# TensorE does the up product of the next expert ahead of the down product of the present one

## What is computed

```
logits = hf @ w_router + b_router
top_logit, top_idx = lax.top_k(logits, TOP_K)
top_w = jax.nn.softmax(top_logit, axis=-1)
def expert_block(args):
    gu = xb @ w_gu[e] + b_gu[e]
    g = jnp.minimum(gu[:, :D_EXPERT], SWIGLU_LIMIT)
    lin = jnp.clip(gu[:, D_EXPERT:], -SWIGLU_LIMIT, SWIGLU_LIMIT)
    glu = g * jax.nn.sigmoid(SWIGLU_ALPHA * g)
    return ((lin + 1.0) * glu) @ w_down[e] + b_down[e]
```

## Time and profile before

| | us |
|---|---|
| runs timed | 1204.57, 1202.98, 1203.69; median 1203.69 |
| the profiled execution, its own time | 1205.13 |
| its span, first to last instruction | 1203.3 |
| TensorE busy | 1110.2 |
| VectorE busy, ScalarE busy | 388.4, 266.0 |

### The profile page before, as it was taken

The page is one execution under the profiler, slowest core; times in us unless marked ns, Lnnn a source line. Parts: engine busy times, 40 slices in busy tenths (PEclk is TensorE's granted clock), DMA queues, the critical chain, the costliest instruction groups (busy, mean ns, idle before and its releaser), DMA issues.

```text
span 1203.3 us, 14750 instructions
## 1 busy us (share of the span) xinstructions
PE 1110.2 (92%) x6099; PEld 587.1 (49%) x6099; DVE 388.4 (32%) x655; ACT 266.0 (22%) x402; POOL 4.5 (0%) x10
## 2 busy tenths in 40 slices
PE   9999999999999998889898888989888999988896
PEld 8999999984433333333333333333333333333332
DVE  6768564563222222222222222222222222222223
ACT  5344674432111111111111111111111111111112
POOL 0000000000000000000000000000000000000000
PEclk9999999999999999999999999999999999999999
DMA  9984344589999999999999999999999999999994
GB/s 331 348 279 141 126 162 165 213 319 372 392 436 427 431 430 429 429 431 432 430 429 431 428 431 430 431 430 430 431 430 432 435 412 426 430 429 430 430 425 158
DMA packets 58826, 452.13 MB, mean 376 GB/s; under 512 B 3314, under 2 KB 34279, under 8 KB 40103
## 3 DMA queue, kind: packets, MB, share of 16 engines
q1 hardware_dynamic: 58112, 449.79, 90.8%
q0 software_dynamic: 560, 1.74, 0.5%
q10 hardware_dynamic: 119, 0.08, 0.0%
HBM read 450.53 MB, written 1.06 MB: 375 GB/s over the span
## 4 chain that ended last, share of the span: by engine, by line
PE 50%; DMA 42%; DVE 4%; ACT 1%; issue 1%; SPq 1%; DVEq 0%; ACTq 0%
DMA dring<-in_w_down_dram 35%; PE bank L1069 17%; PE bank L1362 14%; PE bank L1407 14%; DMA ring<-in_w_gu_dram 6%; DVE region_r L1025 1%; DMA ring<-in_w_mem_kv_dram 1%; PE bank L1389 1%; DVE region_r L1022 1%; DVE region_r L1018 1%; PE bank L1300 1%; DVE region_r L1019 1%; PE bank L1270 1%; PE bank L1159 0%; PE bank L1139 0%
## 5 line engine op out<-in xcount | busy, mean ns | idle before, releaser
L1362 PE MATMUL bank<-ring,region_x 128*64 128x512 f32 x2048 | 449.3, 596 | 10.8 <-DMA ring<-in_w_gu_dram 10.8
L1362 PEld LDWEIGHTS bank<-ring,region_x 128*64 128x64 f32 x2048 | 144.5, 137 | 294.9 <-issue 279.6
L1407 PE MATMUL bank<-dring,region_r 128*64 128x512 f32 x1024 | 237.5, 613 | 45.1 <-DMA dring<-in_w_down_dram 44.3
L1407 PEld LDWEIGHTS bank<-dring,region_r 128*64 128x64 f32 x1024 | 71.9, 140 | 196.4 <-issue 128.0
L1018 DVE TENSOR_SCALAR region_r<-bank 128x512 f32<-128x512 f32 x32 | 22.1, 692 | 364.3 <-PE bank L1362 364.3
L1036 DVE SCALAR_TENSOR_TENSOR y_parts<-bank,region_r,y_parts 64x512 fp32r<-64x512 f32 x32 | 23.8, 744 | 324.2 <-ACT y_parts L630 324.2
L621 ACT ACTIVATE region_r<-region_r 128x512 f32<-128x512 f32 x32 | 20.2, 630 | 417.6 <-DVE region_r L1018 417.6
L1069 PE MATMUL bank<-hT_high,w_high 128*128 128x256 f32 x384 | 110.1, 287 | 0.7 <-DVE hT_low L688 0.7
L1069 PE MATMUL bank<-hT_low,w_high 128*128 128x256 f32 x384 | 108.6, 283 | 0.0
L1069 PE MATMUL bank<-hT_high,w_low 128*128 128x256 f32 x384 | 108.6, 283 | 0.0
L696 DVE TENSOR_TENSOR w_low<-ring,w_high 128x2048 fp32r<-128x2048 f32 x39 | 89.3, 2289 | 53.2 <-ACT w_high L470 53.1
(11 more groups left out here) (240 smaller groups left out, 894.9 us busy)
## 6 DMA issues: line engine op xcount, KB each, us to landing
ring<-in_w_gu_dram SPq DMA_DIRECT2D x54, 4096.0 KB, 27.6
dring<-in_w_down_dram SPq DMA_DIRECT2D x58, 2048.0 KB, 24.5
ring<-in_w_gu_dram SPq DMA_DIRECT2D x18, 2048.0 KB, 10.7
ring<-in_w_in_dram SPq DMA_DIRECT2D x26, 1024.0 KB, 11.9
dring<-in_w_down_dram SPq DMA_DIRECT2D x12, 1024.0 KB, 9.5
ring<-in_w_out_dram SPq DMA_DIRECT2D x4, 1024.0 KB, 4.9
ring<-in_w_gu_dram SPq DMA_DIRECT2D x4, 1024.0 KB, 7.6
ring<-in_w_mem_kv_dram SPq DMA_DIRECT2D x3, 1024.0 KB, 11.5
```

The lines of the kernel that those rows point to most:

```text
L1362: last = mm(ps[64 * half:64 * half + 64, :], xg[u // 2][:, c, 64 * (u % 2):64 * (u % 2) + 64], ring[:, slot0 + c, k * F + half * 512:k * F ...
L1407: last = mm(y_ps[64 * half:64 * half + 64, :], lhsT, dring[:, c // 2, at:at + 512], start=(c == 0), stop=(c == KC - 1))
```

## The change

Expert s's down product now stands behind the up product of s+1. The small products of s (`small_products`: transposes of the hidden values, now in `tr_ps`, transposes of the slot matrix, both halves of the scatter) stand inside up(s+1), behind its third chunk. Behind down(s) come both bias rows for up(s+2) and the gather.

SP's order follows. Its first loads are up 3, then down 1 (in two DMAs, not four); then a loop of up(e+2), down(e); at the end up 28 in halves around down 26, then down 27, up 29, down 28, up 30, down 29, down 30, up 31, `b_down`, down 31. TensorE ends with up 30, down 29, small products, down 30, up 31, `b_down`, hidden transposes, down 31, scatter. The mixer's last piece goes to ring slot 12, waits for the attention values (`y_att_sb`), and thereby frees slot 7 one piece earlier.

```diff
@@ -64,7 +63,7 @@
 
-    return (p + 8 - (N_MIX - MIX_RING)) % MIX_RING
+    return MIX_RING if p == N_MIX - 1 else (p + 8 - (N_MIX - MIX_RING)) % MIX_RING
...
@@ -332,9 +331,10 @@
         for j in range(4):
+            if j == 3:
+                sp.wait_ge(y_att_sb, ATT_H // 2 + X_H)
             mixer_piece(p, a["w_out"][0, j * 256:(j + 1) * 256, :].rearrange("(c p) n -> p c n", p=P), 2)
             p += 1
-        sp.wait_ge(y_att_sb, ATT_H // 2 + X_H)
         sp.dma_start(x_again, a["x"][0].rearrange("(t p) d -> p t d", p=P)).then_inc(x_again_in, 16)
 
...
@@ -370,7 +370,7 @@
             sp.wait_ge(pieces_used, used)
             if n < MIX_RING - 8 and n % 2:
                 up_chunks(0, 8 + n - 1, n - 1, 2)
-            elif n % 2:
+            elif n % 2 and n < MIX_RING - 1:
                 up_chunks(1, n - (MIX_RING - 8) - 1, n - (MIX_RING - 8) - 1, 2)
             if used == N_PROJ + 12:
                 down_slots(0, 2, 1)
@@ -378,6 +378,7 @@
                 down_slots(0, 0, 1)
                 down_slots(0, 1, 1)
             if used == N_MIX - 1:
+                up_chunks(1, 6, 6, 2)
                 up_chunks(0, 14, 6, 2)
             if used == N_MIX:
                 up_chunks(0, 12, 4, 2)
@@ -390,37 +391,33 @@
         for m in range(2, KC // 2):
             sp.wait_ge(pieces_used, N_MIX + 2 * m + 2)
             up_chunks(2, 8 + 2 * m, 2 * m, 2)
-        expert_down(1, 1, 1)
         expert_up(3, 0, N_MIX - RING + 25, 2)
-        expert_down(2, 5)
-        with sp.Fori(1, more * (E // 2) + (E // 2 - 1 - IN_ORDER)) as i:
-            expert_up((i * 2 + 2) % E, 8, i * 16 + (N_MIX - RING + 17))
-            expert_down((i * 2 + 1) % E, i * 8 + 1)
-            expert_up((i * 2 + 3) % E, 0, i * 16 + (N_MIX - RING + 25))
+        expert_down(1, 1)
+
+        with sp.Fori(0, more * (E // 2) + (E // 2 - 4)) as i:
+            expert_up((i * 2 + 4) % E, 8, i * 16 + (N_MIX - RING + 33))
             expert_down((i * 2 + 2) % E, i * 8 + 5)
+            expert_up((i * 2 + 5) % E, 0, i * 16 + (N_MIX - RING + 41))
+            expert_down((i * 2 + 3) % E, i * 8 + 9)
...
-        e0 = E - 2 * IN_ORDER
-        sp.wait_ge(pieces_used, ups + e0 * KC + 3)
-        up_chunks(e0, 8, 0, 4)
-        expert_down(e0 - 1, downs + DRING * (e0 - 1))
-        sp.wait_ge(pieces_used, ups + e0 * KC + 7)
-        up_chunks(e0, 12, 4, 4)
-        expert_down(e0, downs + DRING * e0)
-        expert_up(e0 + 1, 0, ups + (e0 + 1) * KC)
-        expert_down(e0 + 1, downs + (e0 + 1) * DRING)
-        with sp.Fori(1, IN_ORDER - 1) as i:
-            for u in range(2):
-                e = i * 2 + (e0 + u)
-                expert_up(e, 8 * (1 - u), ups + e * KC)
-                expert_down(e, downs + e * DRING)
-        expert_up(E - 2, 8, ups + (E - 2) * KC)
-        expert_down(E - 2, downs + (E - 2) * DRING)
-        expert_up(E - 1, 0, ups + (E - 1) * KC, 2)
-        expert_down(E - 1, downs + (E - 1) * DRING, 1)
-
+        sp.wait_ge(pieces_used, ups + (E - 4) * KC + 3)
+        up_chunks(E - 4, 8, 0, 4)
+        expert_down(E - 6, downs + (E - 6) * DRING)
+        sp.wait_ge(pieces_used, ups + (E - 4) * KC + 7)
+        up_chunks(E - 4, 12, 4, 4)
+        expert_down(E - 5, downs + (E - 5) * DRING)
+        expert_up(E - 3, 0, ups + (E - 3) * KC)
+        expert_down(E - 4, downs + (E - 4) * DRING)
+        expert_up(E - 2, 8, ups + (E - 2) * KC, 2)
+        expert_down(E - 3, downs + (E - 3) * DRING, 1)
+        expert_down(E - 2, downs + (E - 2) * DRING, 1)
+        for c, n in ((0, 2), (2, 2), (4, 2), (6, 1), (7, 1)):
+            sp.wait_ge(pieces_used, ups + (E - 1) * KC + c + n - 1)
+            up_chunks(E - 1, c, c, n)
         sp.wait_ge(pieces_used, more * (KC * E) + (KC * (E - 1) + N_MIX))
         sp.dma_start(b_down, a["b_down"][0]).then_inc(b_down_in, 16)
+        expert_down(E - 1, downs + (E - 1) * DRING, 1)
         sp.dma_start(gain_out, a["norm_final_g"].unsqueeze(0).broadcast_to([P, D])).then_inc(final_gain_in, 16)
...
@@ -614,21 +611,44 @@
...
+        sigmoid_of(0)
+        with act.Fori(0, more * E + (E - 2)) as s:
+            hidden(s)
+            slots(s)
+            sigmoid_of(s + 1)
+            weighted_high(s)
+        hidden(more * E + (E - 2))
+        slots(more * E + (E - 2))
+        weighted_high(more * E + (E - 2))
+        slots(more * E + (E - 1))
+        sigmoid_of(more * E + (E - 1))
+        hidden(more * E + (E - 1))
+        weighted_high(more * E + (E - 1))
...
@@ -1007,37 +1027,62 @@
...
+        def expert_steps(i, last_four):
+
+            for u in range(3 if last_four else 4):
+                s = i * 4 + u
+                if not (last_four and u > 1):
+                    dve.wait_ge(gathered, s + 3)
+                    gathered_half(tr_ps, (u // 2 + 1) % 2, u % 2)
+                    if u % 2 and not last_four:
+                        dve.wait_ge(xg_sb, s + 3)
+                        gather_matrices(s + 3)
+                transposed_slots(s, u)
+                scatter_matrix(s + 1)
+                if not (last_four and u > 1):
+                    activations(s + 1)
+                    bias_selector(s + 2)
+                weighted_low(s)
+
+        dve.wait_ge(gathered, 2)
+        gather_matrices(2)
+        activations(0)
+        bias_selector(1)
...
+        with dve.Fori(0, more * (E // 4) + (E // 4 - 1)) as i:
+            expert_steps(i, False)
+        expert_steps(more * (E // 4) + (E // 4 - 1), True)
+        transposed_slots(more * E + (E - 1), E - 1)
+        activations(more * E + (E - 1))
+        weighted_low(more * E + (E - 1))
...
@@ -1331,95 +1376,131 @@
...
+        def begin(s):
+
+            pe.wait_ge(up_read, s + 1)
+            pe.wait_ge(sel_ready, s + 1)
+            bias_rows(0)
+            bias_rows(1)
+
+        def up(i, u, last_one, between):
+
+            s = i * 4 + u
...
+                for k, ps in enumerate((gate_ps, lin_ps)):
+                    for half in range(2):
+                        last = mm(ps[64 * half:64 * half + 64, :], xg[u // 2][:, c, 64 * (u % 2):64 * (u % 2) + 64],
+                                  ring[:, slot0 + c, k * F + half * 512:k * F + half * 512 + 512],
+                                  start=False, stop=(c == KC - 1))
+                last.then_inc(pieces_used, 1)
+                if c == 2:
+                    between()
+
+        def hidden_transposed(s, halves):
+
+            pe.wait_ge(hid_ready, s + 1)
+            pe.wait_ge(xg_sb, s + halves)
+            for c in range(4):
+                last = transpose(tr_ps[:, c * P:(c + 1) * P], g_sb[:, c * P:(c + 1) * P], ident)
+            last.then_inc(hidT_done, 1)
+
+        def slots_and_scatter(s, u):
+
+            pe.wait_ge(y_ready, s + 1)
+            pe.wait_ge(sca_ready, s + 1)
             for t in range(TT):
-                last = transpose(tr_ps[0:E, t * P:(t + 1) * P], wexp[:, t, 0:E], ident)
-            last.then_inc(wexpT_done, 1)
-
-        def four_experts(i, first_four, last_four):
-
+                last = transpose(y_ps[:, t * P:(t + 1) * P], sca[:, t, :], ident)
+            last.then_inc(scaT_done, 1)
+            pe.wait_ge(scaT_sb, s + 1)
+            for t in range(TT):
+                scatter((u + 1) % 2, t, False)
...
+        def down(s, single):
+
+            pe.wait_ge(hidT_sb, s + 2)
+            pe.wait_ge(scaT_sb, s + 2)
+            pe.wait_ge(w_slot_ready, s + 1)
...
+        def next_half(i, u):
+
+            if u % 2 == 0:
+                pe.wait_ge(gat_ready, i * 2 + (u // 2 + 2))
+            gather(tr_ps, u % 2)
...
+        bias_rows(0)
+        up(0, 0, False, second_half)
+        start_sum(1, 1)
+        pe.wait_ge(weights_sb, 1)
+        for t in range(TT):
+            last = transpose(tr_ps[0:E, t * P:(t + 1) * P], wexp[:, t, 0:E], ident)
+        last.then_inc(wexpT_done, 1)
+        pe.wait_ge(xg_sb, 2)
+        begin(1)
+        pe.wait_ge(wexpT_sb, 1)
+        next_half(0, 0)
+
...
+        with pe.Fori(0, more * (E // 4) + (E // 4 - 1)) as i:
             for u in range(4):
                 s = i * 4 + u
...
-                pe.wait_ge(y_ready, s + 1)
-                pe.wait_ge(sca_ready, s + 1)
-                for t in range(TT):
-                    last = transpose(y_ps[:, t * P:(t + 1) * P], sca[:, t, :], ident)
-                last.then_inc(scaT_done, 1)
-
-                pe.wait_ge(xg_sb, s + 2)
-                if u % 2 == 0:
-                    pe.wait_ge(gat_ready, i * 2 + (u // 2 + 2))
-                if u == 0:
-                    pe.wait_ge(wexpT_sb, 1)
-                gather(tr_ps, u % 2)
-                pe.wait_ge(scaT_sb, s + 1)
-                scatter((u + 1) % 2, 0, False)
-
-                pe.wait_ge(hid_ready, s + 1)
-                for c in range(4):
-                    last = transpose(gate_ps[:, c * P:(c + 1) * P], g_sb[:, c * P:(c + 1) * P], ident)
-                last.then_inc(hidT_done, 1)
-                scatter((u + 1) % 2, 1, False)
-
```

(34 more changed lines are left out.)

155 lines of the change are left out of this document (71 added, 84 removed).

## The result

Four runs of the changed kernel took 1209.77 to 1214.77 us, median **1212.59 us**, beside 1204.13 us for the kernel before on the same chip: ratio 1.0065, 95% interval 1.0053 to 1.0076. The profiled execution took 1212.19 us with a span of 1210.4, which is 7.1 more than before; TensorE is busy 1116.7 us of it, VectorE 392.8, ScalarE 247.3. The change makes the kernel slower by 0.65%; forecast were 0.33%, and 1211.5 us at most.

A forecast was written before the change was run, and what follows sets the result against it. The stream of expert weights was taken to set the pace. Span 1203.3, +2.8 at the end, -1.0 in the opening: 1205.1; with 1.8 outside it and 0.8 for the clock, 1207.7 us; 8-in-10 range 1200.5 to 1211.5.

The forecast's parts named there:

- The middle, nothing: Middle of the expert loop: the weight stream stays unbroken, TensorE only waits longer, 3.7 us per expert; no time gained.
- Waits in the small products covered: Transposes and scatter on TensorE: new waits are covered by other products and priced at nothing, otherwise up to 3 us each.
- rival C: Small products: scatter waits for its own expert's slot matrix, 1.2 us per expert, period 26.7, time 1212.4; chance 0.08.
- The opening, a gain of 1.0: First expert loads: of 3.7 us of stream lost before, 2.7 stay lost in two shallow places, so 1.0 us gained.
- The starting point, 1046.7: Kernel before, landing with 56 MiB of weights still to come: counted back 136.4 us from the last landing at 1183.1.
- The end, the gap: Load queue before down 30: it waits for down 29's slots, so the stream stands still for 5.9 us.
- Rival A: End: TensorE close behind the queue, down 30 follows down 29 without a gap, 1201 in a timed run; chance 0.15.
- The end, from down 29's end to up 31: End: 26.8 us from the end of down 29 to the landing of up 31, of which up 31 takes 19.5.
- Half a clock dip, 0.8 us: New end, where TensorE sets the pace: 0.8 us allowed for half a stay at 1.2 in place of 2.4 GHz.
- three signs: Profile after: no idle DMA stretch in the last 60 us, TensorE waiting in small products, or stream not filled by 345.
- Rival D: Whole kernel: TensorE's idle time sets the time, so losing 22.1 us of hidden-chain waits gives 1181.6; chance 0.02.
- Rival B: Opening: all 3.7 us saved and TensorE's period at 25.34, giving 1204.3, the same time as before; chance 0.13.

The follow-up runs named there:

- experiment 9: The kernel before with only the mixer's last piece in slot 12, its wait moved, slots 6 and 7 filled one piece sooner: 1204.27 us, ratio 0.9998.
- experiment 3: The changed kernel with SP's queue in order of use for the last eight experts, not four: 1209.49 us, ratio 1.0040.
- experiment 5: The kernel of experiment 4 with six experts loaded in order of use in place of eight: 1203.40 us, ratio 0.9992.
- Experiment 10: The changed kernel with down 29, down 30 and all of up 31 in 2 MiB loads: 1217.13 us, ratio 1.0107.
- Experiment 6: The changed kernel with the products of `b_down` behind down 31, as in the kernel before: 1213.12 us, ratio 1.0076.
- second profile: The changed kernel run again unaltered on the same chip, for another profile of its end: 1211.86 us, ratio 1.0065.
- experiment 1: The changed kernel with `bias_selector(1)` ahead of `activations(0)` on VectorE: 1207.6 us, ratio 1.0031.
- experiment 4: The changed kernel with the selector ahead of the activations and the last eight experts loaded in order of use: 1203.12 us, ratio 0.9988.
- experiment 7: The kernel of experiment 4 with `b_down` products ahead of down 30's scatter and their load one place earlier: 1203.18 us, ratio 0.9989.
- experiment 8: The kernel of experiment 7 with TensorE doing products that compute nothing in the bare places of the end: 1201.77 us, ratio 0.9980.

## Why the prediction was half the size

Taken by its own steps, on the first profile:

- **The middle, nothing**: right. 3.7 us of waits per expert were forecast, 2.21 + 1.23 = 3.4 stand in the rows above (the clock in the middle is 0.98 in the mean, which makes an expert there a little longer); the period of TensorE is 25.1, forecast 25.5 (bounds 25.34 to 25.71, so a little under them).
- **Waits in the small products covered**: right in the loop; rival C did not come. Behind the loop, where no up stands between down 29 and the scatter, TensorE waits 2.00 us for the weighting. It costs nothing there, since up 31's weights come later still.
- **The moved mixer piece, 0 us**: right, shown by experiment 9.
- **The opening, a gain of 1.0**: this is the step that failed. A, the landing of down 25, was forecast at 1045.7 and is 1049.9 and 1047.4 in the two profiles. The sentence that broke is "bias rows and gather take it to 302.8". It let TensorE walk through `begin(1)`, which waits for the selector. The cover that the prediction named for VectorE's moved waits, a whole down and more, exists inside the loop; ahead of the loop up 0 is followed directly by `begin(1)`, with no down between them, and the diff shows `activations(0)` ahead of `bias_selector(1)`. Undoing that one line gives 4.3 to 5.0 us by the medians, and 3.7 and 6.2 us on A. With it undone the rest of the forecast for the opening holds: up 1 starts at 302.78 (forecast 302.8), and 24 MiB behind the landing at 310.1 the stream is 0.9 us ahead of the kernel before (371.3 for 372.2; forecast 1.0).
- **The starting point, 1046.7**: also off, and the other way. It was counted back from the last landing at 2.435 us per MiB, as if the stream before ran unbroken to its end. In the profile before, the landing with 56 MiB left is that of the first half of up 27, issued at 1020.2:

```profile
L343 SPq DMA_DIRECT2D ring<-in_w_gu_dram x1: 338/338/338, 1020.2 to 1020.2; - x1
...
DMA to landing us min/median/max: 24.2/24.2/24.2
```

  That is 1044.4, so the last 56 MiB took 138.7 us and not 136.4. A forecast built on it would have been 2.3 us lower and missed by more. With the selector first, A is 1043.67, which is 0.7 below 1044.4. That it is 3.0 below 1046.7 is mostly this error, and no gain of the change.
- **The end, the gap**: right in kind and place. Down 29 ends at A + 104.05 (forecast 105.7), down 30's first load is issued at 1148.8 and lands 5.1 us later:

```profile
L356 SPq DMA_DIRECT2D dring<-in_w_down_dram x1: 328/328/328, 1148.8 to 1148.8; - x1
...
DMA to landing us min/median/max: 5.1/5.1/5.1
```

  By bytes, 253 and 374 GB/s for 433 from 1140 to 1160 are 5.5 us of lost stream; by the landings of the last part of down 29 (1147.8) and of down 30 (1162.1) it is 4.6. Forecast were 5.9, with down 29 ending 1.65 us later than it did. Rival A, a gap that does not open, did not come; experiments 3 and 5 show what opens it.
- **The end, from down 29's end to up 31**: under-sized, 26.8 forecast and 29.65 measured: down 30 has landed after 8.15 us (forecast 7.3), and up 31 takes 21.5 more (forecast 19.5). Experiment 10 has what is known of it. The earlier end of down 29 takes 1.65 off it, so up 31 is done at A + 135.7, not A + 134.2.
- **`b_down` in front and the weighting bare**: right. 3.63, 0.60, the copy, 7.11 and a bare weighting of 3.1 us stand in the chain. Experiment 6 adds that putting `b_down` back is no cure.
- **Half a clock dip, 0.8 us**: the place was wrong. It was taken from a dip behind a wait for weights; what came was a dip in the opening behind the selector wait and, in most kernels with this end, one of 1.3 to 2.7 us on down 31.

The sum, for the first profile: A later by 4.2, the way from A to the last scatter longer by 1.45, what is behind it shorter by 0.35 (9.65 for 10.0), so 1205.1 + 5.3 = 1210.4 us of span. The 4.2 are 6.2 for the selector less 2.3 for the starting point, with 0.3 of rest. In the second profile A is later by 1.7 and the last scatter, at A + 152.1, by 2.7 more, of which 1.7 are down 31 at the low clock. The selector is the largest single error in both, but not the only one. That experiment 1, at 1207.6, meets the forecast of 1207.7 is partly luck: the starting point was 2.3 us too late, and its end, with down 31 at 9.75 us, is longer than forecast.

None of the three signs that the prediction named for being wrong came. The DMA engines stand idle before down 30, nothing waits in the small products of the loop, and the stream is back at 433 GB/s from 330 to 345 us. The fault stood where none of them looked, in the first pass ahead of the loop.

Rival D, by which the time would follow TensorE's idle time, is refuted: the waits for the hidden chain went, and the kernel became slower. Rival B, an opening that gives back more, is not what the runs show either (0.9 us). The Trainium skill (Perfetto Trace Analysis, section Optimization Strategies) gives the use of the matmul engine as the general goal; in this trace TensorE is 100% busy in the stretch from 1140 to 1150 us, in which the stream loses 4.2 us.

## What to carry to other kernels

A cover counted for a loop must be counted again for the first pass: list the waits ahead of the loop one by one and ask on every engine what the awaited instruction is queued behind, also a wait on a third engine and its table load. Read a starting point where it lies in the trace, and don't count it back over a stretch that may have losses of its own. Where a stream of loads is the limit and the order of use changes, look at where the order of the loads changes too: here six experts ahead of the end were enough, and with four the single-buffered down 30 opened a gap of 5.5 us. At the very end small loads were better than pairs here, and behind bare waits of TensorE its clock was low.

## What the runs showed of the chip

The granted clock of TensorE fell to 1.2 GHz at the end of most kernels here, though the last wait for weights ahead of the fall was 0.5 us at most. In experiment 4 it fell during the last of 4.2 us of `b_down` products, of 32 rows and without idle time between them; in experiments 6 and 7 behind bare waits of 3.2 us. Down 31 then took 8.4 to 9.75 us instead of 7.1. In experiment 8, with products of the full 128 rows in the bare places and the 32-row ones ahead of down 30, it was 1.00 from 1177 us on. But in the same profile it was 0.50 from 1150 to 1152, behind the `b_down` products, where in experiment 7 the same instructions left it at 1.00. The first profile of the changed kernel kept its clock with `b_down` ahead of down 31, the second did not. So more decides it than the order of the instructions; what, is open.

A single MiB issued when all before it had landed took 5.1 us in two places (issued at 1148.8 and 1146.3 in the two profiles of after). The third 5.1, at 284.7 in the earlier trace rows, was not on an idle queue, though the prediction says so: the load ahead, issued at 272.1, landed at 287.0, and the same load took 5.4 us in the profile after and 4.9 in that of experiment 1. The price of 5.1 that the sum of the end used is nonetheless what came there. The 4.4 us that the prediction quotes beside it from the Trainium skill (DMA: Bandwidth & Descriptors, section Anatomy of one DMA) are given there for DMAs issued by GpSimd; the loads here are issued by SyncE. The three loads behind the one at 1148.8, issued 1.7 us apart, landed at 3.2, 2.6 and 2.4 us from each other, so the stream was back at its pace of 2.44 with the last of them.
